# Order of ScalarE's work around the attention of the two gated mixers: exponentials before the tanh of z, transposed probabilities before the next weight split

## The chip, the cores and the metric

One Trainium2 chip; the kernel runs on one of its cores. The metric is the device time of one execution in microseconds (us). Engines: PE is TensorE, ACT is ScalarE, DVE is VectorE, POOL is GpSimd, and SP issues the loads.

## The reference, cut to what matters

Two blocks over x of 256 tokens by 1024 channels, all in float32. The first block is an adaptive-norm layer (feed-forward, a mixer of pooling and attention, feed-forward). The second has two attention layers, one with a sliding window and sinks, one causal. The change touches only these two:

```python
h = x
for i in range(2):
    hn = rmsnorm_2(h, norm_g[i])
    q, k, v, z = split_proj(hn, w_in, n_kv)     # 16 heads of 64; 2 or 4 key/value heads
    q, k = apply_rope(q, cos, sin), apply_rope(k, cos, sin)
    o = attention(q, k, v)                      # i = 0: window 128 and sinks; i = 1: causal
    o = o.reshape(B, S, MIX_WIDTH) * jax.nn.silu(z)
    h = h + o @ w_out[i]
```

## The kernel before

Each engine runs one instruction stream in an order written out by hand, and the streams are tied by counting semaphores. A plan (`mixer_plan`) lists the steps of the three mixers, `pool`, `window` and `causal`, and every engine's `mixer(name)` walks the same list. The gated mixers, `window` and `causal`, have four rounds, 0 to 3. Round i handles four heads and has the steps Q{i}, ROTQ, Z{i}, SC{i}. The text calls round i of a mixer "window step i" or "causal step i", up to the values at its end.

- **Weights.** Each unit of weights is 128 x 2048 float32. It is split in two before TensorE can use it: `high` (L554, ACT copies `raw` to `whi`) and `low` (L824, DVE writes `wlo` = `raw` - `whi`). There are three slots (NS = 3), so the split for unit u + 3 can run when unit u has been used. Products are three matmuls per tile (L1154 to L1156).
- **Q and Z (jobs).** Each is a projection of two chunks of 24 matmuls. Between Q's chunks TensorE transposes the probabilities of heads 0 and 1 of the round before (L1291); between Z's chunks it computes the scores of heads 0 and 1 (L1281, L1282), and after Z those of heads 2 and 3 (step SC).
- **SC on DVE.** `masked_max` (L936, ends in `nm`, L943 or L946) for heads 0 and 1, then `gate` (L1021), then `divide` (L953 to L956) and `masked_max` mixed. `gate` makes `sz` = (tanh + 1) * z and raises `z_done`. `divide` scales the exponentials by their reciprocal sum and raises `p_done`, on which the transposes wait.
- **Z and SC on ACT.** The job of Z is the tanh of z (L619), which waits for the end of Z's projection (`job_done`). Then `softmax`: for each head the exponential of the sink (L654, window mixer only) and two exponentials with a sum (L656). Then `high` of the unit three after Z's.
- **What TensorE waits for.** A projection job waits for `z_done` of all Z steps before it (L1221 and L1222), so Q{i+1} starts after the gate of Z{i}; the output product OUTA waits for all gates. `values` (L1303, L1306) waits for the copies of the transposed probabilities to SBUF, `probabilities` on ACT (L663, `pt_done`).
- **After Q's projection.** ACT copies heads 0 and 1 of `probT`, then copies q out of PSUM (L613). In step TPV TensorE does the values of heads 0 and 1 (bank acc), the transposes of heads 2 and 3, the rotation of q, and the values of heads 2 and 3 (bank stat). DVE runs `low` of the unit that ACT split last, then `outputs` (og L969, ylo L974) and the rotary step, on which the next scores wait.
- **The last round** of a gated mixer goes SC3, OUTA, TPV3, OUTB: there the transposes follow the first part of the output product.

Of the kernel before, what the change touches and what calls it, by code (L numbers as in the profile page):

```python
# [32 lines left out]
NS = 3  # L33
# [123 lines left out]
def by_act(a):  # L157

    return (a < MOD_START or 20 <= a < 32) and a % 2 == 1 or a == 22
# [18 lines left out]
def build(nc, x, c, w_ada, b_ada, g_ffn1, w1_gate, w1_up, w1_down, g_mix, w_in, w_pool, pool_scale, w_out,  # L178
          g_ffn2, w2_gate, w2_up, w2_down, g_final, norm_g_2, w_in_a_2, sinks_a_2, w_in_b_2, w_out_2,
          final_g_2, shape_consts, out):  # L180
    with ExitStack() as ctx:
# [365 lines left out]
        def _(act):  # L547
            def high(u, reps=None, by=None):

                if u >= UNITS:  # L550
                    return
                n = 16 * (u // NS + 1)
                act.wait_ge(landed[u % NS], n + 16 * reps if reps is not None else n)
                nc.scalar.activation(whi[:, u % NS], raw[:, u % NS], ACT.Copy).then_inc(hi_done, 1)  # L554
# [89 lines left out]
                        ins = nc.scalar.activation(to, of, ACT.Copy)  # L644
                ins.then_inc(kd_done, 1)

            def softmax(st):
                for n in range(4):
                    h = st["h"] + n
                    s = h % 4  # L650
                    act.wait_ge(nm_done, h + 1)
                    if st["mixer"] == "window":
                        head = st["local"] + n
                        nc.scalar.activation(esink[:, s], nm[:, s], ACT.Exp, bias=sinks[:, head:head + 1])  # L654
                    for b, (lo, up) in enumerate(((0, P), (P, SW))):
                        ins = nc.scalar.activation(prob[:, s, lo:up], prob[:, s, lo:up], ACT.Exp,  # L656
                                                   bias=nm[:, s, b:b + 1], accum_out=den[:, s, b:b + 1])
                    ins.then_inc(ex_done, 1)
# [17 lines left out]
            def mixer(name):  # L676
                before = None
                for st in PLANS[name]:
                    if st["kind"] == "Q" and st["next"]["kind"] == "TPV":
                        probabilities(st["next"], 0)  # L680
                        probabilities(st["next"], 1)
                    if st.get("job"):
                        job(st)
                    elif st["kind"] == "ROTK":
                        duplicate(st)
                    elif st["kind"] == "SC":
                        softmax(st)
                        if before["kind"] == "Z":
                            high(before["u"] + NS)
                    elif st["kind"] == "TPV":  # L690
                        early = before["kind"] == "Q"
                        outputs(st, early)
                        if early:
                            high(before["u"] + NS)
                    elif st["kind"] in ("OUTB", "OUT"):
                        j = st["i"]
                        if name == "causal":
                            act.wait_ge(fin_mm, j + 1)
                        else:
                            k = MIX_NORM[name] + 1  # L700
                            act.wait_ge(delta, DC * RESIDUAL[k] + 2 * j + 2)
                            if j == 0:
                                load_sqrt(k)
                            squares(k, range(2 * j, 2 * j + 2))
                        if j < 3 or name == "causal":
                            high(st["u"] + NS)
                    elif st["kind"] == "MAC":
                        if by_act(st["i"]):
                            product(st["i"])
                        product(st["i"] + 1)  # L710
                    before = st
# [98 lines left out]
        def _(dve):  # L810
# [137 lines left out]
            def divide(st, n):  # L948
                h = st["h"] + n
                s = h % 4  # L950
                dve.wait_ge(ex_done, h + 1)
                if st["mixer"] == "window":
                    link(nc.vector.tensor_tensor(den[:, s], den[:, s], esink[:, s], ALU.add))  # L953
                link(nc.vector.reciprocal(rden[:, s], den[:, s]))
                for b, (lo, up) in enumerate(((0, P), (P, SW))):
                    ins = nc.vector.tensor_scalar(prob[:, s, lo:up], prob[:, s, lo:up], rden[:, s, b:b + 1], None,  # L956
                                                  ALU.mult)
                ins.then_inc(p_done, 1)
# [18 lines left out]
            def mixer(name):  # L977
                before, query = None, None
                for st in PLANS[name]:
                    kind = st["kind"]  # L980
                    if kind == "Q":
                        query = st
                    if st.get("job"):
                        job(st)
                    elif kind in ("ROTK", "ROTQ"):
                        rope(st)
                        if kind == "ROTQ":
                            low(query["u"] + NS)
                    elif kind == "SC":
                        masked_max(st, 0)  # L990
                        masked_max(st, 1)
                        if before["kind"] == "Z":
                            gate(before)
                        divide(st, 0)
                        masked_max(st, 2)
                        divide(st, 1)
                        masked_max(st, 3)
                        divide(st, 2)
                        divide(st, 3)
                        low(before["u"] + NS) if before["kind"] in ("Z", "V") else None  # L1000
                    elif kind == "TPV":
                        outputs(st)
                        if name == "pool" and before["kind"] == "Q":
                            low(before["u"] + NS)
                    elif kind in ("OUTB", "OUT"):
                        if name != "causal":
                            residual(MIX_NORM[name] + 1, range(2 * st["i"], 2 * st["i"] + 2))
                        if st["i"] < 3 or name == "causal":
                            low(st["u"] + NS)
                    elif kind == "MAC":  # L1010
                        reduce_products(st["i"])
                        reduce_products(st["i"] + 1)
                    elif kind == "MOD":
                        mod_out(st["i"])
                    before = st

            def gate(st):

                dve.wait_ge(job_out, st["p"] + 1)
                pair = acc[st["p"] % 2][:, :].rearrange("p (b n) -> p b n", b=2)  # L1020
                nc.vector.scalar_tensor_tensor(out=sz[:, :, :], in0=sz[:, :, :], scalar=1.0, in1=pair, op0=ALU.add,  # L1021
                                               op1=ALU.mult).then_inc(z_done, 1)
# [546 lines left out]
```

## Time and profile before

| what | value |
|---|---|
| time, median of 3 runs | 883.3 us (883.01 to 883.53) |
| the profiled execution | 883.01 us, of which the span of instructions is 881.2 us |
| PE busy | 752.3 us (85%) |
| DVE busy | 609.0 us (69%) |
| ACT busy | 403.3 us (46%) |
| POOL busy | 169.5 us (19%) |
| mean granted clock of TensorE | 0.922 of full |

Full clock is 2.4 GHz, half clock 1.2 GHz. Busy shares are means over the whole kernel. The window mixer runs from about 625 to 747 us of the span, the causal one from about 750 to the end. In rows of a timeline the number in brackets is how long the engine sat idle before that instruction and what ended the wait; equal instructions in a row are merged into one line with their count.

### The profile page before, as it was taken

The page shows a single profiled execution, that of the slowest core. Times are in us where ns is not written, and L with a number is a line of the kernel's source. Part 1 is how long each engine was busy: PE and PEld are TensorE (multiplying, and loading weights), DVE is VectorE, ACT ScalarE, POOL GpSimd, SP SyncE. Part 2 cuts the span into 40 slices and gives each one's busy share as a digit, 9 for nine tenths or more (in the row PEclk, how much of TensorE's full clock was granted, in tenths as well). Part 3 has the DMA queues.
Part 4 walks back from the last instruction along what each step waited for, and adds up shares of the span by engine and source line. Part 5 has one row for each costly group of instructions (what it writes and reads, how often), then busy time and mean ns, then how long its engine had stood idle before and what let it go on. Part 6 is the DMA issues. An engine that isn't in the chain of part 4 may idle for free.

```text
span 881.2 us, 14334 instructions
## 1 busy us (share of the span) xinstructions
PE 752.3 (85%) x5792; PEld 713.0 (81%) x5792; DVE 609.0 (69%) x775; ACT 403.3 (46%) x645; POOL 169.5 (19%) x86
## 2 busy tenths in 40 slices
PE   4269999999969867848999999996798978999984
PEld 3269999999959856647999999996787768878884
DVE  5988777777678888676549557455567775677741
ACT  5454333433437745434443334435365554565542
POOL 3521223422365551234004000001000001000000
PEclk8569999999989988677999999998799999999998
DMA  9877778767673944066567555653133334333201
GB/s 296 281 245 238 247 250 262 233 206 247 228 243 100 330 144 144 29 220 205 182 190 244 197 190 166 200 174 127 48 97 96 122 119 144 112 113 111 96 1 48
DMA packets 132454, 152.61 MB, mean 173 GB/s; under 512 B 2616, under 2 KB 126268, under 8 KB 132284
## 3 DMA queue, kind: packets, MB, share of 16 engines
q1 hardware_dynamic: 132324, 152.01, 52.9%
q8 instruction: 29, 0.48, 0.2%
q14 instruction: 13, 0.11, 0.0%
q10 hardware_dynamic: 88, 0.02, 0.0%
HBM read 150.97 MB, written 1.05 MB: 173 GB/s over the span
## 4 chain that ended last, share of the span: by engine, by line
PE 66%; DVE 16%; ACT 8%; issue 6%; DMA 2%; POOL 1%; SPq 0%; DVEq 0%; POOLq 0%; ACTq 0%
PE sc L1154 10%; PE sc L1155 10%; PE sc L1156 10%; PE acc L1154 8%; PE acc L1155 8%; PE acc L1156 8%; DVE macc L876 6%; ACT whi L554 2%; DVE wlo L824 2%; PE stat L1165 2%; DMA ada<-in_w_ada_dram 2%; ACT prob L656 1%; DVE rstd L844 1%; DVE prob L956 1%; DVE prob L936 1%
## 5 line engine op out<-in xcount | busy, mean ns | idle before, releaser
L824 DVE TENSOR_TENSOR wlo<-raw,whi 128x2048 fp32r<-128x2048 f32 x104 | 252.4, 2430 | 107.5 <-ACT whi L554 107.5
L554 ACT ACTIVATE whi<-raw 128x2048 fp32r<-128x2048 f32 x105 | 199.9, 1905 | 80.1 <-PE sc L1156 71.0
L1154 PE MATMUL sc<-nhi,whi 128*128 128x256 f32 x704 | 203.0, 288 | 10.1 <-DVE nlo L863 6.5
L1155 PE MATMUL sc<-nlo,whi 128*128 128x256 f32 x704 | 201.7, 287 | 0.0
L1156 PE MATMUL sc<-nhi,wlo 128*128 128x256 f32 x704 | 201.5, 286 | 0.0
L468 POOL TENSOR_TENSOR ada<-ada,cT 128x2048 f32<-128x2048 f32 x21 | 99.6, 4743 | 250.5 <-DMA ada<-in_w_ada_dram 250.5
L1154 PEld LDWEIGHTS sc<-nhi,whi 128*128 128x128 f32 x704 | 137.7, 196 | 10.8 <-issue 6.9
L1155 PEld LDWEIGHTS sc<-nlo,whi 128*128 128x128 f32 x704 | 137.8, 196 | 0.0
L1156 PEld LDWEIGHTS sc<-nhi,wlo 128*128 128x128 f32 x704 | 137.7, 196 | 0.0
L1154 PE MATMUL acc<-nhi,whi 128*128 128x256 f32 x376 | 114.5, 305 | 16.5 <-DVE nlo L863 12.1
L876 DVE TENSOR_REDUCE macc<-ada 128x256 f32<-128x2048 f32 x32 | 121.0, 3807 | 5.9 <-POOL ada L468 3.4
L1155 PE MATMUL acc<-nlo,whi 128*128 128x256 f32 x376 | 109.7, 292 | 0.0
L1156 PE MATMUL acc<-nhi,wlo 128*128 128x256 f32 x376 | 109.5, 291 | 0.0
L1154 PEld LDWEIGHTS acc<-nhi,whi 128*128 128x128 f32 x376 | 75.0, 200 | 24.5 <-issue 17.4
L1155 PE MATMUL acc<-hlo,whi 128*128 128x256 f32 x320 | 90.1, 282 | 0.0
L1154 PE MATMUL acc<-hhi,whi 128*128 128x256 f32 x320 | 90.1, 281 | 0.0
L1156 PE MATMUL acc<-hhi,wlo 128*128 128x256 f32 x320 | 90.0, 281 | 0.0
L1155 PEld LDWEIGHTS acc<-nlo,whi 128*128 128x128 f32 x376 | 75.5, 201 | 0.5 <-issue 0.5
L1156 PEld LDWEIGHTS acc<-nhi,wlo 128*128 128x128 f32 x376 | 75.4, 201 | 0.0
L1184 PE MATMUL sc<-ones,macc 128*128 128x1 f32 x92 | 18.2, 307 | 49.5 <-DVE macc L876 39.9
L1155 PEld LDWEIGHTS acc<-hlo,whi 128*128 128x128 f32 x320 | 60.3, 188 | 0.0
L1154 PEld LDWEIGHTS acc<-hhi,whi 128*128 128x128 f32 x320 | 60.3, 188 | 0.0
(163 smaller groups left out, 1265.5 us busy)
## 6 DMA issues: line engine op xcount, KB each, us to landing
ada<-in_w_ada_dram SPq DMA_DIRECT2D x32, 1024.0 KB, 5.2
raw<-in_w_gate_dram SPq DMA_DIRECT2D x22, 1024.0 KB, 5.7
raw<-in_w_up_dram SPq DMA_DIRECT2D x22, 1024.0 KB, 5.4
raw<-in_w_down_dram SPq DMA_DIRECT2D x22, 1024.0 KB, 4.8
raw<-in_w_out_dram SPq DMA_DIRECT2D x12, 1024.0 KB, 4.9
raw<-in_w_in_b_dram SPq DMA_DIRECT2D x10, 1024.0 KB, 5.0
raw<-in_w_in_a_dram SPq DMA_DIRECT2D x9, 1024.0 KB, 5.2
raw<-in_w_in_dram SPq DMA_DIRECT2D x8, 1024.0 KB, 7.7
```

The source lines that it names most:

```text
L468: nc.gpsimd.tensor_tensor(to, to, c_mul, ALU.mult).then_inc(prod_done, 1)
L554: nc.scalar.activation(whi[:, u % NS], raw[:, u % NS], ACT.Copy).then_inc(hi_done, 1)
L656: ins = nc.scalar.activation(prob[:, s, lo:up], prob[:, s, lo:up], ACT.Exp, bias=nm[:, s, b:b + 1], accum_out=den[:, s, b:b + 1])
L824: nc.vector.tensor_tensor(wlo[:, u % NS], raw[:, u % NS], whi[:, u % NS].bitcast(F32), ALU.subtract).then_inc(lo_done, 1)
L844: link(nc.vector.reciprocal(rstd[:, :], std[:, :]))
L876: nc.vector.tensor_reduce(macc[:, slot], src.rearrange("p c n -> p n c"), AX_X, ALU.add).then_inc(macc_done, 1)
L936: ins = nc.vector.tensor_tensor_reduce(out=prob[:, s, lo:up], in0=sc[h % 2][:, lo:up], in1=mask[:, lo:up], scale=1.0, scalar=NEG, op0=ALU. ...
L1154: mm(to, stat_hi, mov_hi, start=first, stop=False, skip_group_check=True)
L1155: mm(to, stat_hi, mov_lo, start=False, stop=False, skip_group_check=True)
L1156: return mm(to, stat_lo, mov_hi, start=False, stop=last, skip_group_check=True)
L1165: mm(ss_ps, ones[:, :], src, start=first, stop=last).then_inc(ss_done, 1)
L1184: ins = mm(to[:, n:n + 1], macc[:, slot, n * P:(n + 1) * P], ones[:, 0:1], start=True, stop=True)
```

## The change

On ACT, in the gated mixers, the step Z no longer does anything. In the step SC the exponentials of heads 0 and 1 come first, then the tanh of z, then the exponentials of heads 2 and 3. The `high` that followed them is held back: where a Q step comes next it is issued after the two copies of `probT` that belong to that Q step, and ahead of the copy of q; where OUTA comes next it stays where it was. On DVE, `divide` of heads 0 and 1 comes before `gate`, and `masked_max` of head 2 after it. The pool mixer, all of TensorE's order, the loads and every count of a semaphore stay as they are.

```diff
--- before.py
+++ after.py
@@ -644,8 +644,8 @@
                         ins = nc.scalar.activation(to, of, ACT.Copy)
                 ins.then_inc(kd_done, 1)
 
-            def softmax(st):
-                for n in range(4):
+            def softmax(st, heads=range(4)):
+                for n in heads:
                     h = st["h"] + n
                     s = h % 4
                     act.wait_ge(nm_done, h + 1)
@@ -679,14 +679,24 @@
                     if st["kind"] == "Q" and st["next"]["kind"] == "TPV":
                         probabilities(st["next"], 0)
                         probabilities(st["next"], 1)
-                    if st.get("job"):
+                        if before["kind"] == "SC" and name != "pool":
+                            high(before["after"] + NS)
+                    if st["kind"] == "Z":
+                        pass
+                    elif st.get("job"):
                         job(st)
                     elif st["kind"] == "ROTK":
                         duplicate(st)
                     elif st["kind"] == "SC":
-                        softmax(st)
                         if before["kind"] == "Z":
-                            high(before["u"] + NS)
+                            softmax(st, (0, 1))
+                            job(before)
+                            softmax(st, (2, 3))
+                            st["after"] = before["u"]
+                            if st["next"]["kind"] != "Q":
+                                high(before["u"] + NS)
+                        else:
+                            softmax(st)
                     elif st["kind"] == "TPV":
                         early = before["kind"] == "Q"
                         outputs(st, early)
@@ -990,10 +1000,14 @@
                         masked_max(st, 0)
                         masked_max(st, 1)
                         if before["kind"] == "Z":
+                            divide(st, 0)
+                            divide(st, 1)
                             gate(before)
-                        divide(st, 0)
-                        masked_max(st, 2)
-                        divide(st, 1)
+                            masked_max(st, 2)
+                        else:
+                            divide(st, 0)
+                            masked_max(st, 2)
+                            divide(st, 1)
                         masked_max(st, 3)
                         divide(st, 2)
                         divide(st, 3)
```

## Rows read from the trace of the kernel before

**Rows 1.** chain of waits in order of time: start us, us, engine, tile, line

```profile
678.46 1.80 ACT whi L554
680.26 0.75 ACT probT L663 x2
683.60 0.58 PE stat L1303 x4
723.99 0.65 PE stat L1303 x4
```

**Rows 2.** timeline, TensorE, window step 1: start us, us, instruction, [idle before it]

```profile
672.36 0.61 PE L1282 MATMUL sc<-kd,qT 64*128 64x256 f32 x4
673.56 0.36 PE L1154 MATMUL acc<-nhi,whi 128*128 128x256 f32 x1 [0.59 <-issue]
676.51 0.49 PE L1291 MATMUL tp<-consts,prob 128*128 128x128 f32 x3
681.06 0.44 PE L1303 MATMUL acc<-probT,vv 128*64 128x256 f32 x2 [0.88 <-ACT probT L663]
```

**Rows 3.** timeline, ScalarE, window step 1

```profile
672.14 0.60 ACT L619 ACTIVATE sz<-acc 128x512 f32<-128x512 f32 x1 [4.67 <-PE acc L1156]
672.63 0.29 ACT L654 ACTIVATE esink<-nm,sinks 128x2 f32<-128x2 f32 x1
673.70 0.28 ACT L654 ACTIVATE esink<-nm,sinks 128x2 f32<-128x2 f32 x1
```

**Rows 4.** timeline, VectorE, window step 1

```profile
670.84 0.23 DVE L943 TENSOR_SCALAR nm<-mx,sinks 128x2 f32<-128x2 f32 x1
672.77 0.69 DVE L1021 SCALAR_TENSOR_TENSOR sz<-sz,acc 128x512 f32<-128x512 f32 x1 [0.89 <-ACT sz L619]
673.83 0.16 DVE L953 TENSOR_TENSOR den<-den,esink 128x2 f32<-128x2 f32 x1 [0.37 <-ACT prob L656]
674.68 0.29 DVE L936 CUSTOM_DVE_ANT_0 prob<-sc,consts 128x128 f32<-128x128 f32 x1
```

**Rows 5.** timeline, VectorE, window step 0, second gated output

```profile
664.79 0.42 DVE L969 SCALAR_TENSOR_TENSOR og<-stat,sz 128x256 f32<-128x256 f32 x1 [0.37 <-PE stat L1306]
```

**Rows 6.** timeline, VectorE then TensorE, window step 0

```profile
649.95 0.23 DVE L943 TENSOR_SCALAR nm<-mx,sinks 128x2 f32<-128x2 f32 x1
652.97 0.69 DVE L1021 SCALAR_TENSOR_TENSOR sz<-sz,acc 128x512 f32<-128x512 f32 x1 [1.99 <-ACT sz L619]
661.40 0.65 PE L1303 MATMUL acc<-probT,vv 128*64 128x256 f32 x4 [1.02 <-ACT probT L663]
```

**Rows 7.** timeline, TensorE, window output step

```profile
717.23 0.49 PE L1291 MATMUL tp<-consts,prob 128*128 128x128 f32 x3
720.39 1.12 PE L1303 MATMUL acc<-probT,vv 128*64 128x256 f32 x4 [2.34 <-ACT probT L663]
```

**Rows 8.** granted clock by stretch: PE, PEld, DVE, ACT, POOL busy, PEclk, DMA

```profile
720.20:723.60 3.40, 3.02 (x14) 1.91 (x14) 2.14 (x2) 0.78 (x3) 0.00 (x0) 0.50 0.13 36
```

**Rows 9.** timeline, VectorE then ScalarE, causal step 1

```profile
797.59 0.17 DVE L946 TENSOR_SCALAR nm<-mx 128x2 f32<-128x2 f32 x1
799.51 0.69 DVE L1021 SCALAR_TENSOR_TENSOR sz<-sz,acc 128x512 f32<-128x512 f32 x1 [1.00 <-ACT sz L619]
799.37 0.39 ACT L656 ACTIVATE prob<-prob,nm 128x128 f32<-128x128 f32 x1
800.25 0.39 ACT L656 ACTIVATE prob<-prob,nm 128x128 f32<-128x128 f32 x1
```

**Rows 10.** timeline, TensorE, causal steps 0 and 1

```profile
788.14 0.20 PEld L1303 LDWEIGHTS acc<-probT,vv 128*64 128x64 f32 x4 [0.34 <-ACT probT L663]
806.92 0.44 PE L1303 MATMUL acc<-probT,vv 128*64 128x256 f32 x2
```

**Rows 11.** timeline, TensorE then ScalarE, causal output step

```profile
844.01 0.49 PE L1291 MATMUL tp<-consts,prob 128*128 128x128 f32 x3
844.53 0.49 ACT L663 ACTIVATE probT<-tp 128x384 f32<-128x384 f32 x1 [0.85 <-PE tp L1291]
```

## The prediction

> **What bounds the kernel now.** I read three views in this order. First the chain of waits, to see which engines the end hangs on in the two gated mixers. In window step 1 it runs through ACT: exponentials, then a weight split of 1.80 us, then two copies of `probT` in 0.75 us, and only then TensorE's values [rows 1]. Then TensorE's timeline, because it is the engine that has to be kept going: it shows two holes in each round. One stands before the next Q projection: scores of heads 2 and 3 end at 672.97 and Q starts at 673.56 [rows 2]. The other stands before the values, 0.88 us on the copies [rows 2]. Then ACT and DVE at these places, to see what ends each hole. Q starts 0.10 after the gate's end (672.77 + 0.69 = 673.46) [rows 2, 4], so the first hole belongs to `z_done`. The second belongs to the split that stands ahead of the copies [rows 1]. The change attacks the second hole and puts work in front of the gate, which ends the first. That is the whole case: a gain at the values against a loss at Q's start.
>
> **The loss: the gate comes later.** New order on ACT: exp 0, exp 1, tanh. In window step 1 the first `nm` ends at 670.84 + 0.23 = 671.07 [rows 4], long before tanh could start at 672.14 [rows 3], and ACT had idled 4.67 us. So exp 0 starts at 671.10. One head takes 1.07 (672.63 to 673.70 [rows 3]), so exp 1 starts at 672.17 and tanh at 673.24; the gate followed tanh's start by 0.63 (672.14 to 672.77 [rows 3, 4]), so by ACT it could start at 673.87. But DVE now does two divides first. A divide starts 1.20 after its exponential's start (672.63 to 673.83) and the next DVE instruction follows 0.85 later (673.83 to 674.68) [rows 3, 4]: divide 1 runs from 673.37 to 674.22. The gate starts at 674.22 in place of 672.77: 1.45 later, and Q with it. Behind the gate on DVE are `masked_max` 2 and 3; they start near 674.8 and 675.7, as now (674.68 [rows 4]), so exp 3 ends near 677.9. Q's transposes then start at 676.51 + 1.45 = 677.96 [rows 2], so ACT is just free for the copies. Window step 2 repeats this to 0.01.
>
> In window step 0 nothing holds the scores up: `nm` 0 ends at 650.18 [rows 6], exp 0 and 1 start at 650.21 and 651.28, divide 1 ends at 652.48 + 0.85 = 653.33, and the gate moves from 652.97 [rows 6] by 0.36.
>
> In the causal steps there is no sink exponential: one head takes 0.88 (799.37 to 800.25 [rows 9]), a divide about 0.85 less the 0.16 of the sink's addition [rows 4] = 0.69. `nm` 0 ends at 797.76 [rows 9]: exp 0 at 797.80, exp 1 at 798.68, divide 1 from 798.68 + 0.88 + 0.13 = 799.69 to 800.38. The gate moves from 799.51 [rows 9] by 0.87; I take 0.85. Causal step 0 has the same early scores as window step 0 and shorter exponentials: between 0 and 0.36, I take 0.
>
> **The gain: the values don't wait for the split.** With the copies first, they are over 1.3 us after the transposes start (0.52 from transpose to copy [rows 11], then 0.75 [rows 1]), while Q's second chunk still runs. The hole goes: 1.02 in window step 0 [rows 6], 0.88 in steps 1 and 2 [rows 2]. In causal step 0 at most 0.34, I take 0.2; in causal steps 1 and 2 no idle is shown, so nothing [rows 10].
>
> What is late next: the split, and `low` behind it. The split now ends 680.26 - 681.06 = -0.80, so 0.80 ahead of the values' start [rows 1, 2]. After the change it ends 0.52 + 0.75 + 1.80 = 3.07 behind the transposes' start, and the values start 681.06 - 0.88 - 676.51 = 3.67 behind it: 0.60 ahead. So `low` ends some 0.2 later against the values than now, 0.4 if the transposes' copies start a little later. Behind `low` on DVE stand both gated outputs and the rotary step, on which Z's scores wait. The cover is that DVE waits 0.37 for TensorE before the second output [rows 5]. So it is just hidden, and costs 0 to 0.1 a step if not; I take 0. ACT's copy of q comes after the split and still starts with Q's end, so it costs nothing. The loads that wait for `low` have two units of slack. No DMA, no SP and no POOL instruction is moved.
>
> **Output steps.** In the window mixer OUTA starts 1.45 later, so its transposes start at 717.23 + 1.45 = 718.68 [rows 7], the copies at 719.20, and the values 0.90 after that (two copies of 0.75 and the wait), 720.10 against 720.39 [rows 7]: 0.3 gained, since the wait of 2.34 covered the gate's delay. That wait has a second effect. Behind it TensorE's granted clock was 0.50 for 3.4 us, 720.2 to 723.6 [rows 8]: that is 1.2 GHz in place of 2.4, and the engine had been idle since about 718. From first to second values took 720.39 to 723.99, 3.60, against 681.06 to 683.60, 2.54 in step 1 [rows 1, 2, 7]. With the wait down to 0.6 this goes: 1.06 gained. In the causal mixer ACT waits for the transposes, 0.85 [rows 11]; TensorE is not held by ACT there, and the delay of 0.85 counts in full.
>
> **The clock behind the new holes.** In window steps 1, 2 and the output step, TensorE will be idle from 672.97 to 675.01: 2.04 us, where the trace of before has 0.59 at that place [rows 2]. Idle of 2.34 brought the clock down [rows 7, 8], idle of 1.02 did not [rows 6]. The new 2.04 is nearer to the upper one, and whether it falls will vary from hole to hole and from run to run. One stretch of 3.4 us at half clock costs between 1.06 (as above) and 1.7 (half of 3.4); I take 1.3, since dense projections fill it. I count one stretch in three holes. The causal holes, 0.59 + 0.85 = 1.44, are nearer to 1.02: none.
>
> The Trainium skill, page "TensorE: Matmul & The Clock Gate", section "Why this matters for your kernels", advises only against gaps longer than this one; by that advice the clock would hold in all three holes and the sum would be 1.3 lower. The row of 2.34 speaks against relying on it: by this kernel's trace a gap that is also within that advice was followed by half clock.
>
> **The sum**, against the profiled execution's own 883.01: window step 0, 0.36 - 1.02 = -0.66; steps 1 and 2, 1.45 - 0.88 = +0.57 each; window output -0.30 and clock -1.06; causal step 0 -0.20; causal steps 1, 2 and output +0.85 each. Together +1.47. One stretch of low clock +1.3. 883.01 + 2.77 = 885.8 us. The median of the runs shown is 883.3, 0.3 above the profiled one, so this is +2.5 on the median (+0.28%).
>
> **Rivals.**
> - *The clock holds.* Same holes, no low stretch: 884.5, or +1.2 on the median, within 0.2%. For it: TensorE ran at full clock through every hole up to 1.02. Against: the row of 2.34.
> - *Two or three low stretches, or `low` no longer hidden:* +1.3 to +2.6, and 0.1 in each of six steps: 887.1 to 888.9.
> - *Faster: the gate does not hold Q.* If Q's start hangs on something that stays, only the gains are left: 1.02 + 0.88 + 0.88 + 0.2, the output's end on the earlier exponentials 0.4, the clock 1.06: 4.4, which gives 878.6. It decides where the gate's delay falls under 0.88 a window step. For it: TensorE's idle before Q is marked as issue, not as a wait for DVE [rows 2]. Against: Q starts 0.10 after the gate's end, and the code makes it wait for `z_done`.
> - *Nothing happens.* ACT is busy 46% of the span. The rule would be that reordering an engine with half its time idle moves nothing, since both holes are only exchanged: 883.0 to 883.6. Against: in four of eight steps the two sides differ by 0.57 or more. The Trainium skill, page "Perfetto Trace Analysis", section "Identifying the Most-Contended Engine", would have one work on the engine with the highest occupancy first; by it this change is worth nothing, and [rows 1] shows why the share misleads: the chain passes through ACT.
> - *The tables.* If exp and tanh needed different tables, two reloads a step would come on top, over 5 us in all: 891 and more. Against: they alternate in all eight steps already.
>
> **Chances.** Forecast with one low stretch or so, 885.1 to 886.9: 0.48. Clock holds: 0.22. Two or more, or `low` exposed: 0.14. Gate does not hold Q: 0.08. Nothing: 0.05. Tables or another stall: 0.03. The range takes in the first three: 884.0 to 888.6. A measurement of this kernel can tell about 0.2%, 1.8 us, from no change: slower is the forecast, the third and the last case, 0.65; same is the clock case and nothing, 0.27; faster 0.08.
>
> **What would show it.** In window steps 1 and 2: gate about 2.1 after the end of Z in place of 0.6, Q 1.4 to 1.5 later, no idle before the values, `low` ending 0.2 to 0.4 later against them, the rotary step as far behind the values as now. In causal steps 1 and 2: Q 0.85 later, values without idle as before. Stretches of clock 0.50 inside Q2, Q3 or OUTA of the window mixer, and none at its TPV3. Wrong would be: a gate that starts right behind tanh, a Q that starts ahead of the gate, or scores of Z that come later against the values.

## The result, and the profile after

The changed kernel takes 887.94 us (median of five runs, 886.19 to 889.15) against 883.46 for the kernel before in runs beside it (883.01 to 884.59). The ratio is 1.0048, with a 95% interval of 1.0034 to 1.0061: slower by half a per cent. The time lies inside the predicted range and 2.1 us above the predicted 885.8. The profiled execution took 886.19 us.

The page of the kernel after, first its span, then the busy time of each engine:

```profile
span 884.3 us, 14334 instructions
...
PE 755.2 (85%) x5792; PEld 716.8 (81%) x5792; DVE 608.6 (69%) x775; ACT 404.0 (46%) x645; POOL 169.9 (19%) x86
```

Busy time tells little: ACT and DVE have the same work as before (404.0 and 608.6 us against 403.3 and 609.0). The hole ahead of Q is on TensorE's timeline, window step 1 (start, duration, the instruction; in brackets the idle time before it):

```profile
670.21 0.61 PE L1296 MATMUL sc<-kd,qT 64*128 64x256 f32 x4
...
672.86 0.36 PE L1168 MATMUL acc<-nhi,whi 128*128 128x256 f32 x1 [2.04 <-issue]
...
676.89 0.84 PE L1305 MATMUL tp<-consts,prob 128*128 128x128 f32 x3
...
680.96 0.65 PE L1317 MATMUL acc<-probT,vv 128*64 128x256 f32 x4
```

Scores end at 670.21 + 0.61 = 670.82 and Q starts at 672.86, after 2.04 us of idle; before, the same place had 0.59 [rows 2]. The values at 680.96 wait for nothing, where they waited 0.88 before [rows 2]. Both are as predicted to a hundredth. ACT at the same place shows the new order, exponentials of heads 0 and 1, tanh, and the split only after the copies:

```profile
668.95 0.30 ACT L654 ACTIVATE esink<-nm,sinks 128x2 f32<-128x2 f32 x1 [3.63 <-DVE nm L953]
...
670.03 0.28 ACT L654 ACTIVATE esink<-nm,sinks 128x2 f32<-128x2 f32 x1
...
671.09 0.57 ACT L619 ACTIVATE sz<-acc 128x512 f32<-128x512 f32 x1
...
677.77 0.49 ACT L663 ACTIVATE probT<-tp 128x384 f32<-128x384 f32 x1 [1.93 <-PE tp L1305]
678.20 0.49 ACT L663 ACTIVATE probT<-acc 128x384 f32<-128x384 f32 x1
678.59 1.90 ACT L554 ACTIVATE whi<-raw 128x2048 fp32r<-128x2048 f32 x1
```

and DVE the divide that now stands ahead of the gate (`den` is its first instruction), the gate, and `low`:

```profile
671.22 0.16 DVE L963 TENSOR_TENSOR den<-den,esink 128x2 f32<-128x2 f32 x1
...
672.08 0.68 DVE L1035 SCALAR_TENSOR_TENSOR sz<-sz,acc 128x512 f32<-128x512 f32 x1
...
680.52 2.29 DVE L834 TENSOR_TENSOR wlo<-raw,whi 128x2048 fp32r<-128x2048 f32 x1 [3.70 <-ACT whi L554]
```

The gate follows tanh by 0.99 (671.09 to 672.08), where it was 0.63 [rows 3, 4], and tanh itself starts after two heads of exponentials, so Q goes from 0.59 to 2.04 behind the scores. The gate ends at 672.76, and Q starts 0.10 later, the same distance as before [rows 2, 4].

Behind the hole the clock fell. The view by stretches has, for each, its length, then the busy time (and count) of PE, weight loads, DVE, ACT and POOL, then the granted clock, the DMA share and GB/s:

```profile
674.40:677.80 3.40, 3.40 (x19) 3.40 (x18) 1.75 (x8) 1.47 (x8) 0.00 (x0) 0.50 0.02 5
...
677.80:681.20 3.40, 3.40 (x29) 3.22 (x29) 0.68 (x1) 2.83 (x4) 0.00 (x0) 1.00 0.00 0
...
694.90:698.30 3.40, 3.40 (x19) 3.40 (x18) 2.65 (x16) 2.23 (x10) 0.00 (x0) 0.50 0.03 7
```

Two stretches of 3.4 us at 0.50, one in step 1 and one in step 2, both behind a hole: the first starts 1.5 us after the hole of 2.04 has ended, the second 0.3 after that of 2.06. The first has 19 matmuls in it, the next stretch at 1.00 has 29. At the output step the reverse took place: the values wait 0.63, not 2.34 [rows 7],

```profile
722.02 0.65 PE L1317 MATMUL acc<-probT,vv 128*64 128x256 f32 x4 [0.63 <-ACT probT L663]
```

and the low stretch there [rows 8] is gone; from first to second values 2.31 us passed in place of 3.60.

In the causal mixer, step 1, the same two marks, PE and then DVE:

```profile
802.13 0.35 PE L1168 MATMUL acc<-nhi,whi 128*128 128x256 f32 x1 [1.41 <-ACT sz L619]
...
808.68 0.65 PE L1317 MATMUL acc<-probT,vv 128*64 128x256 f32 x4
```

```profile
798.59 0.17 DVE L956 TENSOR_SCALAR nm<-mx 128x2 f32<-128x2 f32 x1
...
801.35 0.68 DVE L1035 SCALAR_TENSOR_TENSOR sz<-sz,acc 128x512 f32<-128x512 f32 x1
```

The gate started 1.92 behind `nm` of head 0 before (797.59 to 799.51 [rows 9]) and starts 2.76 behind it now (798.59 to 801.35). Q waits 1.41 ahead of its start. The values have no idle, as before [rows 10], so here nothing is given back.

A table of the time from one round's first values to the next round's puts this together, with the runs that follow. It is worked out from the start of the values (L1303 before, L1317 after) in each timeline, in us. "3 to causal 0" is the way from the output step of the window mixer to the first values of the causal one:

| profile | window 0 to 1 | 1 to 2 | 2 to 3 | 3 to causal 0 | causal 0 to 1 | 1 to 2 | 2 to 3 |
|---|---|---|---|---|---|---|---|
| before | 19.66 | 19.66 | 19.66 | 67.76 | 18.78 | 18.77 | 19.76 |
| after | 21.71 | 21.67 | 19.39 | 67.13 | 19.53 | 19.54 | 20.58 |
| copies_first | 19.86 | 19.69 | 20.64 | 66.86 | 18.95 | 18.81 | 19.84 |
| exps_first | 21.71 | 21.67 | 19.56 | 67.06 | 19.55 | 19.56 | 20.59 |
| gate_first | 20.31 | 20.34 | 20.82 | 66.61 | 19.37 | 19.35 | 20.41 |
| filled_hole | 20.17 | 20.16 | 19.40 | 66.72 | 19.56 | 19.55 | 20.59 |
| q_free | 18.15 | 19.23 | 22.25 | 66.81 | 18.09 | 18.19 | 20.69 |
| q_free_before | 19.67 | 19.66 | 19.65 | 67.11 | 18.78 | 18.77 | 19.77 |
| gate_last | 18.07 | 18.20 | 19.76 | 70.47 | 18.07 | 18.08 | 19.75 |
| gate_last_split | 18.15 | 18.14 | 19.67 | 70.50 | 18.07 | 18.07 | 19.75 |
| mixed_last | 18.14 | 18.15 | 21.00 | 66.24 | 18.07 | 18.08 | 19.76 |
| mixed_last_filled | 18.14 | 18.14 | 19.63 | 65.42 | 18.07 | 18.08 | 19.75 |
| after_again | 21.69 | 21.68 | 19.41 | 67.30 | 19.54 | 19.54 | 20.58 |

One stretch of low clock that no wait of the change touches moves the fourth column. TensorE is idle for 4.0 us ahead of the causal mixer in every profile. Behind it, before and then after:

```profile
750.80:754.20 3.40, 3.40 (x18) 3.40 (x18) 3.40 (x10) 2.15 (x5) 0.00 (x0) 0.51 0.02 5
754.20:757.60 3.40, 3.40 (x30) 3.40 (x30) 1.90 (x5) 2.71 (x3) 0.00 (x0) 0.98 0.00 0
```

```profile
747.40:750.80 3.40, 0.00 (x0) 0.00 (x0) 3.08 (x5) 0.97 (x3) 0.00 (x0) 0.81 0.38 130
750.80:754.20 3.40, 3.22 (x15) 3.25 (x16) 3.40 (x10) 2.03 (x4) 0.00 (x0) 0.50 0.02 5
754.20:757.60 3.40, 3.40 (x23) 3.40 (x23) 1.90 (x6) 2.82 (x3) 0.00 (x0) 0.69 0.00 0
```

That is 3.4 us of half clock before and 6.8 after. From the end of that idle to the next one 19.85 us pass before and 20.71 after, 0.86 more. The longer form also stands in *copies_first* and *q_free_before*, which keep the old order of exponentials, tanh and gate, so it is not the new order's doing.

### The profile page after: what moved, and what is told of

The parts are those of the page before. It is cut to its first block, busy times and chain, and to the rows that moved or that the text cites. A ratio compares the mean times of both kernels' runs of the same rounds, so it can differ in the third digit from the quotient of the medians.

```text
span 884.3 us, 14334 instructions
## 1 busy us (share of the span) xinstructions
PE 755.2 (85%) x5792; PEld 716.8 (81%) x5792; DVE 608.6 (69%) x775; ACT 404.0 (46%) x645; POOL 169.9 (19%) x86
## 4 chain that ended last, share of the span: by engine, by line
PE 66%; DVE 17%; ACT 7%; issue 6%; DMA 2%; POOL 1%; SPq 0%; DVEq 0%; POOLq 0%; ACTq 0%
PE sc L1168 10%; PE sc L1170 9%; PE sc L1169 9%; PE acc L1168 9%; PE acc L1170 8%; PE acc L1169 8%; DVE macc L886 6%; DVE wlo L834 3%; PE stat L1179 2%; DMA ada<-in_w_ada_dram 2%; ACT whi L554 1%; ACT prob L656 1%; DVE rstd L854 1%; DMA raw<-in_w_gate_dram 1%; PE tp L1305 1%
## 5 line engine op out<-in xcount | busy, mean ns | idle before, releaser
L1168 PEld LDWEIGHTS acc<-nhi,whi 128*128 128x128 f32 x376 | 76.8, 204 | 29.4 <-issue 23.6
L1170 PEld LDWEIGHTS acc<-hhi,wlo 128*128 128x128 f32 x320 | 60.2, 188 | 0.0
```

What stands on the lines that cost most here:

```text
L1168: mm(to, stat_hi, mov_hi, start=first, stop=False, skip_group_check=True)
L1170: return mm(to, stat_lo, mov_hi, start=False, stop=last, skip_group_check=True)
```

## The experiments

Times are medians; each ratio is against runs of the kernel before beside it, with its 95% interval.

### Two halves of the change

*copies_first* is the kernel before with only the held-back split, *exps_first* the kernel after without it.

```diff
 copies_first, on the kernel before:
                         probabilities(st["next"], 1)
+                        if before["kind"] == "SC" and name != "pool":
+                            high(before["after"] + NS)
... (and the old place of high goes, unless OUTA comes next)
 exps_first, on the kernel after:
-                        if before["kind"] == "SC" and name != "pool":
-                            high(before["after"] + NS)
... (and high stands behind the exponentials again)
```

In *exps_first* the split follows the exponentials at once, as before.

> The kernel before with one part of the change: the weight split after Z is held back behind the two copies of the transposed probabilities; exponentials, tanh and gate keep their old order. Theory A (the two holes are independent): the holes of 1.02, 0.88 and 0.88 us before the values go, nothing is lost, about 880.5 us. Theory B (the split and DVE's low half behind it are the next thing late): the copies can't start before the exponentials end (678.36 in window step 1), so the split ends 0.75 later than before in absolute time; DVE covers 0.37 of it, and the rotary step and Z's scores come 0.4 later in each of window steps 0 to 2 and 0.3 later in causal steps 0 to 2: 885 to 886 us, with the hole before the values closed and a larger hole in the middle of Z.

Measured: 883.62 us, ratio 1.0001 (0.9988 to 1.0014). TensorE and DVE of *copies_first*, behind Q1 in the window mixer:

```profile
678.86 0.65 PE L1307 MATMUL acc<-probT,vv 128*64 128x256 f32 x4
...
681.34 0.65 PE L1307 MATMUL stat<-probT,vv 128*64 128x256 f32 x4
```

```profile
679.78 2.29 DVE L828 TENSOR_TENSOR wlo<-raw,whi 128x2048 fp32r<-128x2048 f32 x1 [1.60 <-ACT whi L554]
...
681.99 0.42 DVE L973 SCALAR_TENSOR_TENSOR og<-acc,sz 128x256 f32<-128x256 f32 x1
...
685.80 0.69 DVE L926 TENSOR_TENSOR qT<-tn 128x512 f32<-128x512 f32 x1
```

The values' wait on the copies is gone, yet the step is not shorter: 19.86 and 19.69 against 19.66. DVE idles 1.60 for `whi`, and `low` ends at 679.78 + 2.29 = 682.07, 3.2 behind the start of the values; in the kernel before it ended 1.5 behind it. The gated outputs and the rotary step queue behind `low`: `qT`, the last of the rotary step, starts 6.94 behind the values (678.86 to 685.80), against 5.96 before. So the 0.88 that the values gain is lost at the scores of Z, which wait for `qT`. The gain of this half is real and goes nowhere. Neither expected time came: the mechanism is that of theory B, but its 885 to 886 was too high. In step 0 the values gain 1.1 (from the rotation 15.89 in place of 16.99), the steps behind keep that, and only the output step, 20.64 against 19.66, takes it back.

> The kernel after without the held-back split: exponentials of heads 0 and 1 ahead of tanh and both divides ahead of the gate, the split right behind the exponentials as in the kernel before. Theory A (holding back the split is what closes the hole before the values): the hole stays and the gate's delay comes on top, +1.45 a window step and +0.85 a causal step, 891 us or more. Theory B (Q starts so late that the copies are through by then anyway, since the exponentials end 0.4 earlier): values at the same place as in the kernel after, same time as after, 887 to 888 us, and low half done earlier against the values.

Measured: 888.25 us, ratio 1.0047 (1.0028 to 1.0066), the ratio of the whole change. Its steps are those of after to 0.02, apart from the output step (19.56 against 19.39). ACT, window step 1:

```profile
677.84 1.90 ACT L554 ACTIVATE whi<-raw 128x2048 fp32r<-128x2048 f32 x1
...
679.86 0.49 ACT L663 ACTIVATE probT<-tp 128x384 f32<-128x384 f32 x1
```

With the exponentials done earlier the split ends at 679.74, 0.76 behind the start of the transposes, and the copies follow it; they end at 680.77, while the values are due only at 683.05, with Q's second chunk before them. The copies start 0.88 behind the transposes, as they do in after (676.89 to 677.77). In step 0, where the split does hold them up, they start 1.75 behind, and the values have no idle there either. So the whole loss comes with the order of exponentials, tanh and gate, and the held-back split adds nothing to it.

### The gate's place on DVE

*gate_first* keeps ACT's new order and puts the gate back ahead of the divides.

```diff
                         if before["kind"] == "Z":
-                            divide(st, 0)
-                            divide(st, 1)
                             gate(before)
-                            masked_max(st, 2)
-                        else:
-                            divide(st, 0)
-                            masked_max(st, 2)
-                            divide(st, 1)
+                        divide(st, 0)
+                        masked_max(st, 2)
+                        divide(st, 1)
```

> The kernel after with VectorE's old order: the gate directly behind tanh, then divide 0, masked_max 2, divide 1. If the gate's end sets Q's start and the two divides ahead of it cost 0.35 in window steps 1 to 3, 0.36 in window step 0 and 0.17 in causal steps 1 to 3: gate 0.63 behind tanh's start, hole before Q 1.7 us instead of 2.0, 1.9 us faster than the kernel after, and fewer stretches of half clock behind it: 885 to 886.5 us. If something else holds Q, no difference to after (887.9).

Measured: 885.4 us (883.53 to 887.4), ratio 1.0021 (1.0008 to 1.0035). More than half of the loss is back. The window steps are 20.31 and 20.34, with no stretch of 0.50 in them; the causal ones 19.37 and 19.35, 0.6 above before. What remains is ACT's part. DVE stands at the gate, on a tanh that comes two heads later, and the divides queue behind it:

```profile
673.59 0.69 DVE L1031 SCALAR_TENSOR_TENSOR sz<-sz,acc 128x512 f32<-128x512 f32 x1 [1.97 <-ACT sz L619]
```

The split and `low` are late too: `low` ends 2.8 behind the start of the values, and the rotary step 0.5 later than before. The next section gives 20.16 for a window step of after without the low clock. Against that, 20.3 is no gain: what comes back in the window steps is the clock, behind holes of 1.68 in place of 2.04, and the old place of the gate itself gives only the 0.17 in each causal step.

### Is it the clock?

*filled_hole* is the kernel after with 12 matmuls whose result nobody reads, placed behind the scores of heads 2 and 3 in the window mixer, ahead of Q. They add work and change no order.

```diff
+            def filler(st):
+                done = st["next"]["next"]["g"]
+                pe.wait_ge(og_done, done)
+                for n in range(12):
+                    mm(stat[:, 0:S], nhi[:, 0, 0:P], nhi[:, n % DC], start=True, stop=True)
...
                             scores(st, (2, 3) if before["kind"] in ("Z", "V") else range(4))
+                            if name == "window":
+                                filler(st)
```

> The kernel after with 12 extra matmuls of 128x256 on TensorE behind the scores of heads 2 and 3, in the window mixer alone; their result is not used. They take about 1.4 us of the hole of 2.04 us, so they delay nothing. If half clock follows from the idle hole: no stretch of clock 0.50 in the window mixer's Q2, Q3 and OUTA, steps 1 and 2 last 20.2 to 20.3 us each in place of 21.7, runs closer together, 884.5 to 885.5 us. If the low clock there has another cause, the stretches stay and the time is that of after (887.9) or more.

Measured: 885.73 us (883.21 to 887.36), ratio 1.0026 (1.0014 to 1.0038). TensorE at the hole of window step 1, and the stretch behind it (the same stretch of after has 0.50 and 19 matmuls):

```profile
671.26 1.69 PE L1421 MATMUL stat<-nhi 128*128 128x256 f32 x12
...
673.38 0.35 PE L1168 MATMUL acc<-nhi,whi 128*128 128x256 f32 x1 [0.42 <-issue]
```

```profile
674.40:677.80 3.40, 3.40 (x31) 3.40 (x30) 2.23 (x11) 2.92 (x13) 0.00 (x0) 1.00 0.02 5
```

The twelve matmuls take 1.69 us, Q's own wait is 0.42, and it starts at the gate as before. The clock stays at 1.00, 31 matmuls fit where 19 did, and the steps are 20.17 and 20.16 in place of 21.71 and 21.67. So the idle of TensorE, and not the work itself, brings the clock down, and one stretch costs 1.5 us. By itself the delay of the gate costs 20.16 - 19.66 = 0.50 a step. The median is 2.2 us under that of after and 2.5 under that of *exps_first*, which ran beside it, where the two steps of the profiles give 3.0; it is slightly above the expected 884.5 to 885.5. All runs together bear the clock out: their mean granted clock is 0.924 in *filled_hole* (12 runs) and 0.921 in *exps_first* (8). One stretch of 3.4 us at half takes 0.0019 off the mean over 885 us, so an execution of *filled_hole* has on average 1.6 such stretches less, an estimate that at 1.5 us each gives 2.4.

### Is it the gate that holds Q?

A projection waits for the gate of every Z before it, and Q{i+1} does not read what the gate of Z{i} makes. In *q_free* (on after) and *q_free_before* (on before) Q waits for the gates of earlier rounds only.

```diff
-                if st["zs"]:
-                    pe.wait_ge(z_done, st["zs"])
+                zs = st["zs"] - (kind == "Q")
+                if zs > 0:
+                    pe.wait_ge(z_done, zs)
```

> The kernel after, with one wait less on TensorE: a Q projection waits for the gates of the rounds before, not for the gate of the Z ahead of it (Q and Z use different banks, so it needs no data from it); the output product still waits for all gates. If the late gate is what the change loses by: Q starts right behind the scores, 1.9 us earlier in window steps 1 and 2, no stretch of half clock there, values 1.4 us earlier than in the kernel before. The next thing late is then the low half behind the held-back split, about 3.2 us behind the values where more than 2.2 delays the rotary step: window steps 19.1 us each in place of 21.7, causal steps 18.5 in place of 19.5, together 881 to 882 us. If the gate is not the cause, the steps stay at 21.7 and 19.5.

> The kernel before with the same wait taken away. Theory: here the gate holds Q by 0.6 us only, and that gives nothing, since the values still wait for the split and the copies, which hang on ScalarE's exponentials: same steps of 19.7 and 18.8 us, 883 to 884 us. If the wait for the gate is worth something by itself whatever ScalarE's order, it is 0.6 us in each of six steps: 880.3 us.

Measured: *q_free* 882.07 us (880.74 to 883.05), ratio 0.9983 (0.9974 to 0.9992); *q_free_before* 883.21 us, 0.9998 (0.9987 to 1.0009). On the changed kernel the edit is worth 5.9 us by the medians (5.7 by the ratios), on the one before nothing. In the first, Q follows the scores at once, and the window steps fall to 18.15 and 19.23 (the second with `low` 3.4 behind the start of the values), the causal ones to 18.1 and 18.2. The expectation had 19.1 and 18.5, so it was right in the total and too high in all steps but that one; the rest went at the output step, below. TensorE of *q_free*:

```profile
671.85 0.61 PE L1297 MATMUL sc<-kd,qT 64*128 64x256 f32 x4
...
672.39 0.38 PE L1168 MATMUL acc<-nhi,whi 128*128 128x256 f32 x1
```

In *q_free_before* the values wait longer for ACT instead, 1.16 in place of 0.88, and the step is 19.66 as before:

```profile
680.18 0.65 PE L1304 MATMUL acc<-probT,vv 128*64 128x256 f32 x4 [1.16 <-ACT probT L663]
```

So the gate holds Q. Before the change the exponentials behind tanh, the split and the copies stood right behind that on ACT, and freeing Q showed nothing. In *q_free* 22.25 us pass to the output step: OUTA, which does need all gates, now takes the hole, with a low stretch behind it at 714.5.

### Gate last

If Q needs no gate, the gate can stand behind everything on DVE. *gate_last* is *q_free* with the gate behind `masked_max` 3 in rounds 0 to 2, and the old order of tanh and gate in round 3, where OUTA waits for the gate. *gate_last_split* is the same without the held-back split.

```diff
                         if before["kind"] == "Z":
-                            softmax(st, (0, 1))
-                            job(before)
-                            softmax(st, (2, 3))
+                            if st["next"]["kind"] == "Q":
+                                softmax(st, (0, 1))
+                                job(before)
+                                softmax(st, (2, 3))
+                            else:
+                                job(before)
+                                softmax(st)
...
+                        late = before["kind"] == "Z" and st["next"]["kind"] == "Q"
+                        if before["kind"] == "Z" and not late:
+                            gate(before)
                         divide(st, 0)
                         masked_max(st, 2)
                         divide(st, 1)
                         masked_max(st, 3)
+                        if late:
+                            gate(before)
... (and Q's wait as in q_free)
```

> The change with its loss taken out: exponentials first and copies ahead of the split as in the kernel after; Q does not wait for its own gate; on VectorE divide 0, masked_max 2, divide 1, masked_max 3, then the gate, in rounds 0 to 2; in round 3 of each mixer the gate and tanh first as in the kernel before, since the output product waits for it. Exponentials of heads 2 and 3 end about 1 us earlier than in q_free, so the low half ends about 2.1 us behind the values and delays nothing. Window steps 18.2 us in place of 19.7 before, causal steps 18.1 in place of 18.8: 877 to 878.5 us, below both kernels. If the split's lateness still counts: 879 to 881.

> gate_last with the split directly behind the exponentials, as in the kernel before, so without the second half of the change. Now that Q starts early, the copies come due before the split ends: they start at 6.5 us behind tanh's old start in place of 4.7, the values at about 7.4 to 7.5 in window steps and later than gate_last by up to 0.3. If holding back the split is worth something once the gate is out of the way, gate_last is faster by 0.5 to 1.5 us; if not, the two are the same.

Measured: 879.97 us (879.15 to 881.62), ratio 0.996 (0.9944 to 0.9976), and 879.96 us (878.69 to 881.07), 0.9963 (0.9949 to 0.9978). Both are faster than before, but two microseconds short of what the first was to bring. The steps are 18.1 to 18.2 in both mixers, as expected. The missing part stands at the output step of the window mixer, in *gate_last*: the values wait 2.21, and the clock is low on both sides of 722:

```profile
717.03 0.65 PE L1321 MATMUL acc<-probT,vv 128*64 128x256 f32 x4 [2.21 <-ACT probT L663]
```

```profile
718.00:722.00 4.00, 3.42 (x17) 2.26 (x16) 1.74 (x4) 1.47 (x4) 0.00 (x0) 0.51 0.56 184
...
722.00:726.00 4.00, 3.50 (x17) 3.26 (x16) 1.18 (x3) 2.18 (x5) 0.00 (x0) 0.50 0.23 78
```

It is low for 10.2 us in all, not 3.4, and from these values to the causal ones 70.47 us pass, where 67 is usual. The held-back split, for which the expectation left 0.5 to 1.5 open, is worth nothing here either.

### Each mixer in its own order

*mixed_last* is *gate_last_split* with the order of after in the window mixer's round 3 alone (exponentials first, and the gate behind the divides of heads 0 and 1), which keeps the values' wait short there; *mixed_last_filled* adds the twelve unused matmuls ahead of that OUTA.

```diff
-                            if st["next"]["kind"] == "Q":
+                            if st["next"]["kind"] == "Q" or name == "window":
                                 softmax(st, (0, 1))
                                 job(before)
                                 softmax(st, (2, 3))
... (and the order of divide and gate on DVE)
 mixed_last_filled, besides:
+                            if name == "window" and st["next"]["kind"] == "OUTA":
+                                filler(st)
```

> gate_last_split with one more edit: the last round of the window mixer takes the order of the kernel after (exponentials and divides ahead of the gate), that of the causal mixer keeps the old one. In the profile of gate_last_split the wait of 2.2 us before that round's values was followed by 10.2 us of half clock and the time from there to the causal mixer was 3 us longer. If that is the clock: the wait shrinks to 0.6, these 3 us go unless the hole before the output product (2.0 us) takes the clock down instead: 878 us with a spread of 2 us. If those 3 us were lost to something else (a load, a dependence), 880.

> mixed_last with 12 unused matmuls of 128x256 on TensorE in the hole before the window mixer's output product, so that neither hole of that round is long. Clock account: no half clock between 700 and 740 us, 877 us. Other account (the hole's length doesn't matter there): as mixed_last.

Measured: *mixed_last* 877.78 us (875.56 to 878.13), ratio 0.9933 (0.9919 to 0.9946), the lowest median of all and 5.8 us under the 883.54 of the kernel before beside it. The way from the output step to the causal mixer is back at 66.24. It still has one low stretch, at 708.7, behind the hole ahead of OUTA:

```profile
708.64 0.52 PE L1172 MATMUL acc<-yhi,whi 128*128 128x256 f32 x1 [2.20 <-DVE sz L1039]
```

*mixed_last_filled*: 878.25 us (874.52 to 878.9), ratio 0.9939 (0.9925 to 0.9953). Its profile has no low stretch between 700 and 740 and is the shortest seen, 874.52, but the median is not better. Whether the filling pays over many executions stays open.

### The change once more

*after_again* is the changed kernel, for the clock's behaviour in a second profile.

> The kernel after once more, beside the variants: its time moves with how many of the three holes of 2.0 us in the window mixer are followed by half clock. By the account so far: window steps of 20.2 us without and 21.7 with such a stretch, causal steps 19.5 in every execution, 885.5 to 889, median 887 to 888. If the two long steps of the first profile (21.7) are fixed and not a matter of the clock, they show 21.7 again wherever the clock is full.

Measured: 888.22 us (886.93 to 889.2), ratio 1.0054 (1.0041 to 1.0068). The low stretches are again two, at 674.7 and 695.1, and *exps_first*, with the same order, has two as well, at 676.5 and 697.0.

## Why the prediction was right, and where its sizes were off

**Bound and direction: right.** The case was a gain at the values against a loss at Q. *q_free* and *q_free_before* show both holes to be what the prediction took them for, and the rival in which the gate does not hold Q falls: the timeline marks the 2.04 us as "issue", but freeing Q from the gate takes 5.9 us off. "Nothing happens" falls with the ratio. Two readings in that rival were off: the two sides differ by 0.57 or more in six of the eight steps of the sum, not in four, and TensorE with its 85% is the busiest engine, so going by the busiest engine leads to its holes and does not make the change worth nothing. The rival of different tables falls with the unchanged busy time of ACT.

**The window holes: right.** Predicted +0.57 for each of steps 1 and 2 without clock, measured 0.50 in *filled_hole*. Predicted idle 2.04, measured 2.04. Step 0, from the rotation to its values, was 16.99 and is 16.25: -0.74 against -0.66. Output step -0.27 against -0.30.

**The causal steps: right, 0.03 to 0.1 too large.** 0.75, 0.77 and 0.82 against 0.85 each; causal step 0, from the rotation to its values, is -0.20 as predicted. At the output step the prediction had TensorE not held by ACT; its values do wait 0.63 for the copies, before and after, but the copies follow the transposes, so the delay counts in full all the same.

**`low` stays hidden: right, but for a bound that was too small.** In after `low` ends at 680.52 + 2.29 = 682.81, 1.9 behind the start of the values, against 1.5 before: 0.3 to 0.4 later, the predicted upper figure, and it costs nothing. The cover was read as 0.37 from DVE's wait [rows 5]. *copies_first*, *gate_first* and *q_free*, whose `low` ends 3.2, 2.8 and 3.4 behind the start of the values, have the rotary step 1.0, 0.5 and 1.2 later behind them than before: always the excess over 2.24. So `low` may end 2.24 behind the start of the values before anything is later, and the cover is 2.24 - 1.53 = 0.7. With the split moved alone, as in *copies_first*, this decides the case.

**The clock: the step that failed.** The prediction counted "one stretch in three holes" at 1.3, and a credit of 1.06 for the stretch that goes at the output step. The charge was mis-sized in count and in price: two stretches, each in three of three profiles of this order, at 21.7 - 20.16 = 1.5 us. That is 3.0 in place of 1.3. The third hole, ahead of OUTA, was a little longer and was not followed by one:

```profile
716.39 0.36 PE L1168 MATMUL acc<-yhi,whi 128*128 128x256 f32 x1 [2.21 <-DVE sz L1035]
```

Behind it the granted clock was 1.00 up to 721.2, where in *mixed_last* a hole of 2.20 at the same place did bring it down. The credit was mis-sized the other way: in the pair of profiles it is 1.29 (3.60 less 2.31), but it is due only when the kernel before has that stretch, and of three profiles with its wait of about 2.3 at the output step (before, *q_free_before*, *copies_first*) only the first has it. The other two have a stretch instead in the causal output step, where the kernel before has none. In *copies_first*:

```profile
848.40:851.80 3.40, 3.40 (x17) 3.40 (x18) 0.00 (x0) 1.29 (x1) 0.00 (x0) 0.50 0.02 5
```

From the last round's values to the end both take 37.3 in place of 35.8. So a single profile was read as the rule.

**The sum again**, with what the runs showed: -0.74 + 2 x 0.50 - 0.27 - 0.20 + 0.75 + 0.77 + 0.82 = 2.1 without clock, where the prediction had 2.53 without it. Two stretches add 3.0, or 2.5 by the medians of *filled_hole*, and a third of 1.29 goes off: an estimate of 4.2 to 4.7, and the medians differ by 4.5 (this result), 4.7 (*after_again*) and 4.3 (*exps_first*). The two profiled executions differ by 3.2. There the full 1.29 comes off, the part before the window mixer, which the change does not touch, was 1.4 shorter, and the longer low clock ahead of the causal mixer adds 0.86: 3.3. So it was luck that the profiled 886.19 came within 0.4 of the predicted 885.8, since the 1.7 that the new stretches were short of was made up in good part by the 1.4 ahead of the window mixer, which the sum does not have, and by smaller errors.

The prediction's rival of two or three stretches (887.1 to 888.9, 0.14) is thus what took place; the forecast had its mechanism and its sign, and its size only through a wide range.

The Trainium skill, page "TensorE: Matmul & The Clock Gate", section "Why this matters for your kernels", would have let the clock hold in all these holes. Here two of three holes of 2.04 to 2.21 us were followed by half clock, and filling them kept it full, so the measurement decides against the advice as a safe bound.

## What to carry to other kernels

When two edits each remove a wait, ask for each alone what is late next: here putting the exponentials first cost time while Q waited for the gate (*exps_first*, 1.0047), and freeing Q gained nothing while the exponentials stood behind tanh (*q_free_before*, 0.9998), though both together, with the gate last, gave 1.5 us a step (19.66 to 18.1, *gate_last_split*). The held-back split was worth nothing in any pair of runs. A semaphore that waits for more than its reader needs is the first thing to narrow, since it then allows any order behind it. On TensorE, price a new idle gap at the gap plus the half-clock stretch it may bring, and count such stretches in several profiles before a term rests on one.

## What the hardware showed that was not expected

- Half clock comes in stretches of 3.4 us behind idles of 2.04 us (after, *after_again*, *exps_first*), but not behind each: the idle of 2.21 ahead of OUTA in after is of the same kind and the clock held. Nor is one long idle needed: in *copies_first* the stretch at 848.4 stands behind idles of 0.63, 0.64 and 0.90 us, a place where the clock held in before. Which holes are followed by half clock is not settled here. In *gate_last* and *gate_last_split* the low clock lasted 10.2 us behind a wait of 2.2.
- One 3.4 us stretch costs 1.5 us where projections fill it, a little under half of its length.
- Unused matmuls of 1.69 us in a hole of 2.04 did not delay Q and took 1.5 us a step off (*filled_hole*); at another hole the gain did not show in the median (*mixed_last_filled*).
